# GpSimd in place of VectorE for the low parts of six projection weights in a two-layer attention kernel

## The reference, cut to what matters

```
h = modulate(rms_norm(x, norm1_g[i]), sh1, sc1)
hc = modulate(rms_norm(ctx, norm1_g[i]), csh1, csc1)
a_z, bq, bk, bv, cq, ck, cv = split_proj(h @ w_in[i])      # w_in[i]: 1024 x 2048
a_zc, bqc, bkc, bvc, cqc, ckc, cvc = split_proj(hc @ w_in[i])
...                       # roots, gains and rotations of bq, bk, cq, ck
s = einsum(q_c, k_c) ; p = softmax(s) ; pd = p[0] - lam * p[1] ; o = pd @ v   # "C" heads
out_b = window_attn_latent(q_b, k_b, v_b, k_bc, v_bc, b_sink[i])              # "B" heads
```

## Time and profile before

| | us |
|---|---|
| median of 3 runs (lowest, highest) | 1688.5 (1685.79, 1691.37) |
| the profiled execution, its own time | 1696.3 |
| its span in the profile | 1694.5 |
| PE busy | 1646.9 (97%) |
| DVE busy | 1213.6 (72%) |
| ACT busy | 880.1 (52%) |
| POOL busy | 200.2 (12%) |

### The profile page before, as it was taken

The page is one execution under the profiler, slowest core; times in us unless marked ns, Lnnn a source line. Parts: engine busy times, 40 slices in busy tenths (PEclk is TensorE's granted clock), DMA queues, the critical chain, the costliest instruction groups (busy, mean ns, idle before and its releaser), DMA issues.

```text
span 1694.5 us, 34323 instructions
## 1 busy us (share of the span) xinstructions
PE 1646.9 (97%) x14687; PEld 1470.6 (87%) x14687; DVE 1213.6 (72%) x2054; ACT 880.1 (52%) x1335; POOL 200.2 (12%) x124
## 2 busy tenths in 40 slices
PE   8999999999999999999989999999999998899999
PEld 7999988898999999997766888888887786699999
DVE  3374499687777786577766788876888778568864
ACT  5435645548546665445774444323433456656643
POOL 4303540000000110100000111100110100131100
PEclk9999999999999999999999999999999999999999
DMA  7655555354455554521202243363344322045544
GB/s 273 243 210 222 195 218 184 152 222 174 148 176 178 189 174 155 183 102 54 73 2 85 91 149 136 144 229 138 135 160 176 131 76 101 5 172 186 188 160 139
DMA packets 41128, 259.65 MB, mean 153 GB/s; under 512 B 4368, under 2 KB 7696, under 8 KB 14480
## 3 DMA queue, kind: packets, MB, share of 16 engines
q1 hardware_dynamic: 40976, 257.46, 42.3%
HBM read 256.39 MB, written 1.05 MB: 152 GB/s over the span
## 4 chain that ended last, share of the span: by engine, by line
PE 76%; DVE 17%; ACT 3%; DMA 2%; issue 2%; SPq 0%; DVEq 0%; ACTq 0%
PE acc_psum L197 22%; PE acc_psum L199 21%; PE acc_psum L198 21%; DVE w_low_sb L163 3%; DVE mod_products L324 2%; PE acc_psum L2511 2%; PE acc_psum L206 2%; DVE ring_sb L324 2%; PE acc_psum L2537 1%; DVE u_filtered L2064 1%; PE acc_psum L260 1%; ACT w_high_sb L152 1%; DMA ring_sb<-in_w_up 1%; ACT norm_rt_sb L2761 1%; PE acc_psum L1098 1%
## 5 line engine op out<-in xcount | busy, mean ns | idle before, releaser
L197 PE MATMUL acc_psum<-h_high_sb,w_high_sb 128*128 128x256 f32 (+1 forms) x2176 | 664.3, 305 | 4.5 <-DVE h_low_sb L486 2.6
L199 PE MATMUL acc_psum<-h_high_sb,w_low_sb 128*128 128x256 f32 (+1 forms) x2176 | 658.7, 303 | 0.0
L198 PE MATMUL acc_psum<-h_low_sb,w_high_sb 128*128 128x256 f32 (+1 forms) x2176 | 658.3, 303 | 0.0
L152 ACT ACTIVATE w_high_sb<-ring_sb 128x1024 fp32r<-128x1024 f32 (+2 forms) x412 | 386.9, 988 | 375.6 <-PE acc_psum L199 230.3
L163 DVE TENSOR_TENSOR w_low_sb<-ring_sb,w_high_sb 128x1024 fp32r<-128x1024 f32 (+1 forms) x358 | 391.0, 1134 | 109.9 <-ACT w_high_sb L152 100.3
L197 PEld LDWEIGHTS acc_psum<-h_high_sb,w_high_sb 128*128 128x128 f32 x2176 | 411.4, 189 | 33.0 <-issue 12.0
L198 PEld LDWEIGHTS acc_psum<-h_low_sb,w_high_sb 128*128 128x128 f32 x2176 | 410.8, 189 | 17.6 <-issue 0.5
L199 PEld LDWEIGHTS acc_psum<-h_high_sb,w_low_sb 128*128 128x128 f32 x2176 | 411.1, 189 | 17.2
L163 POOL TENSOR_TENSOR w_low_sb<-ring_sb,w_high_sb 128x1024 fp32r<-128x1024 f32 x54 | 131.9, 2465 | 682.0 <-ACT w_high_sb L152 681.9
L2064 DVE SCALAR_TENSOR_TENSOR u_filtered<-acc_psum,par_sb,u_filtered 128x255 f32<-128x255 f32 (+2 forms) x264 | 150.7, 571 | 58.3 <-ACT u_filtered L2201 40.3
L197 PE MATMUL acc_psum<-u_high,w_high_sb 128*128 128x256 f32 (+1 forms) x528 | 169.2, 320 | 3.3 <-DVE w_low_sb L163 2.8
(11 more groups left out here) (312 smaller groups left out, 1872.2 us busy)
## 6 DMA issues: line engine op xcount, KB each, us to landing
ring_sb<-in_w_in SPq DMA_DIRECT2D x68, 1024.0 KB, 6.4
ring_sb<-in_w_up SPq DMA_DIRECT2D x66, 1024.0 KB, 4.9
ring_sb<-in_w_down SPq DMA_DIRECT2D x48, 704.0 KB, 4.1
ring_sb<-in_w_ada SPq DMA_DIRECT2D x24, 1024.0 KB, 4.8
ring_sb<-in_w_ada_rows SPq DMA_DIRECT2D x24, 1024.0 KB, 4.8
ring_sb<-in_w_out SPq DMA_DIRECT2D x12, 1024.0 KB, 4.8
ring_sb<-in_w_br_hg SPq DMA_DIRECT2D x4, 1024.0 KB, 6.9
ring_sb<-in_w_br_ml SPq DMA_DIRECT2D x4, 1024.0 KB, 5.0
```

Source lines behind the costliest of these rows:

```text
L152: self.nc.scalar.activation(self.high[:, g % 2, piece], self.ring[:, c % RING, piece], ACT.Copy)\
L197: nc.tensor.matmul(out, sh, mh, start=start, stop=False)
L198: nc.tensor.matmul(out, sh, ml, start=False, stop=False)
L199: return nc.tensor.matmul(out, sl, mh, start=False, stop=stop)
```

## The change

In both attention layers the units g = 2 to 7 (7, 4, 2, 3, 1, 0) get the word "pool", and a block for POOL is added that runs their `split_low` in order. Unit g = 0 is still POOL's, g = 1 and g = 8 are still DVE's. DVE's calls stay in the code and do nothing for the six units. Nothing else changes: ACT, PE and SP have the same instructions in the same order.

```
         for i in range(LAYERS):
-            add("w_in_2", [8 * i + n for n in (6, 5, 7, 4, 2, 3, 1, 0)], "dve", "pool")
+            add("w_in_2", [8 * i + n for n in (6, 5)], "dve", "pool")
+            add("w_in_2", [8 * i + n for n in (7, 4, 2, 3, 1, 0)], "pool", "pool")
...
             sp.wait_ge(*ws_in.at(16))
 
+        @block.gpsimd
+        def _(pool):
+            for g in range(2, len(ORDER)):
+                core.split_low(pool, g0 + g, "pool")
+
         @block.tensor
```

## The result

The changed kernel takes 1708.2 us (median of 4 executions, 1704.3 to 1708.4), the kernel before 1689.9 us on the same chip (4 executions, 1685.8 to 1691.4): ratio 1.0102, 95% interval 1.0077 to 1.0126. It is slower, by about 1%. The forecast of 1701.8 us had the right sign and its range of 1689 to 1709 holds the time, but the time is 6.4 us above it, and 2.2 us above the 1697 to 1706 that the walk gave for itself.

A forecast was written before the change was run, and what follows sets the result against it. PE's matmuls bound the kernel; only 5.0 us of waits for DVE could be won. Place by place, 3.2 + 0 + 1.6 + 0.7 + 2.9 + 4.9 = 13.3 us on the 1688.5 us median gave 1701.8 us, range 1689 to 1709.

The forecast's parts named there:

- the walk: Both attention layers, DVE's timeline place by place: POOL's L163 hold DVE's instructions, 13.3 us slower, 1701.8 us; chance 0.58.
- D (relief): Both attention layers: all 5.0 us of PE's waits for DVE go and nothing is held, 1683.5 us; chance 0.04.
- C (only the pace): POOL and DVE do not hold each other off, slack covers POOL's pace: -3 to +0.5, 1688 us; chance 0.12.
- A (small instructions slip through, or their delay is covered): Only holds of long instructions cost, 3.2 + 2.9: +6.1 us, 1694.6 us; chance 0.16.
- B (pile-up): g = 4 and 5 also cost, 2.9 us a layer, other places hit at worst phase: +22, 1710.6 us; chance 0.10.
- the sum of 13.3 us: PE's added standing time over both attention layers, relief already taken off: 3.2 + 0 + 1.6 + 0.7 + 2.9 + 4.9.
- Layer 0, g = 2 and 3: Two POOL pairs hold DVE 9.5 us, L2934 ends 4.4 us later, PE stands 3.2 us at the transposes.
- Layer 0, g = 4 to 7: 0 at g = 4 and 5 (covered by waits for scores), 1.6 us at g = 6, 0.7 us at g = 7.
- Layer 1, g = 2 and 3: L2934 ends 4.4 us later, 1.5 us of cover before PE's transposes, PE stands 2.9 us.
- Layer 1, g = 6 and 7: Softmax chain, `mix` and the rotations of `keys_b` held; L2925 4.9 us late, 3.8 the other way, and PE waits.

The follow-up runs named there:

- the dummies: Kernel before, plus POOL products of two constant tiles into scratch that nobody waits for: 1733.4 us, ratio 1.0245; with memsets that only write instead: 1693.1 us, 1.0006.
- g = 6 and 7 alone: Changed kernel with only the low parts of units 1 and 0 left on POOL, the other units' back on DVE: 1696.3 us, ratio 1.0031 to the kernel before.
- g = 4 and 5 together: Changed kernel with only the low parts of units 2 and 3 left on POOL, the other units' back on DVE: 1691.9 us, ratio 1.0018 to the kernel before.
- the kernel with memsets: Kernel before, plus four POOL memsets of a 128 x 512 scratch tile for each high piece of g = 2 to 7: 1693.1 us, ratio 1.0006.
- the two kernels with fillers: Unused constant matmuls put in PE's waits: kernel before, three waits of layer 1, 1689.7 us, 0.9983; changed kernel, all long waits, 1698.7 us, 1.0047 to before.

## Why the prediction was right, and by how much it was off

The mechanism is the one predicted: what DVE is relieved of is less than what POOL's reading holds it up, and PE waits for DVE at the named places. The rivals fall. D (relief) and C (only the pace) are excluded by the sign and by the dummies. A (small instructions slip through, or their delay is covered) by the 2.28 us of a 128 x 1 instruction and by the 1.0031 of g = 6 and 7 alone; the 35 us that it took as free on DVE in each layer are 40 in layer 0. B (pile-up) gave nearly the timed size, but for another reason: g = 4 and 5 together cost 1.5 to 3 us and not 5.8, and the parts add up without a pile-up.

How the sum of 13.3 us fared, step by step. Net of the clock, as above, layer 0 is 187.3 us before and 191.9 after, layer 1 133.0 and 139.5. Other traces repeat this: 191.7 and 139.3 in the second trace of the changed kernel, 187.3 and 133.1 in that of the kernel with memsets.

- *Layer 0, g = 2 and 3*: 3.2 us predicted; 2.1 at the transposes and 0.2 at the low part measured. The four holds added 2.08 + 2.19 us for each unit, 8.5 us and not 9.5, since DVE's instruction comes to POOL's piece when it has run for 0.3 to 0.4 us; and the second piece of g = 2 was nearly in time. Counted from the layer's first L450 and net of the clock, L2940 ends 3.8 us later than L2934 did, where 4.4 was predicted.
- *Layer 0, g = 4 to 7*: 2.3 us predicted (0 + 1.6 + 0.7). `values` waits 2.5 us more, `turn` 0.6 us less. In sum layer 0 is 4.6 us longer, 5.5 predicted.
- *Layer 1, g = 2 and 3*: 2.9 predicted, 1.9 measured, for the same reason (L2940 is 3.2 us late and not 4.4).
- *Layer 1, g = 6 and 7*: 4.9 predicted. `turn` waits 3.6 us, where I had 4.1, and not the same two were held: the walk had L2962 (now L2968) held by the first piece and L2972 (now L2978) by the second. L2968 slipped through at 1412.00, 0.16 us ahead of POOL's start, and L2978 and `mix` were held in their place. For that case the walk had a stall of 1.4 us with `mix` alone held, which was too little, so that the 4.1 came nearly true is in part luck. The B transposes wait 4.4 us, and the 2.4 us of `values` are down to 0.2. The layer is 6.5 us longer, 7.8 predicted; less the 1.9 above, that leaves 4.6 for this step.

So the stalls came to 4.6 + 6.5 = 11.1 us where the sum had 13.3. The holds were sized 1 us too long for each pair of units in `keys_c`, and the rest was close.

What the sum did not have is a term: **the clock of TensorE behind the stalls**. Each us of wait was counted once. But the profile before already had it: its windows show a granted clock of 0.98 and 0.96, which nothing in the prediction used, and finer windows put part of it right behind the 2.4 us wait in layer 1, with 0.83 from 1415 to 1425 us:

```profile
1415.00:1425.00 10.00, 7.64 (x105) 7.06 (x104) 9.59 (x25) 6.01 (x11) 0.00 (x0) 0.83 0.24 75
```

Over all executions the changed kernel loses 15.6 us to the clock and the one before 11.1, 4.5 us more. Of the difference of the mean times (1706.6 over 8 executions, 1691.0 over 49: 15.6 us), 11.1 are the stalls, and 4.5 are left, as much. In the first result, 18.3 us, the medians of 4 executions each lie 1 to 2 us on the far side of these means. That every us at the lower clock costs a us is not shown: over the 49 executions of before the time rises by 0.78 us for each us lost (correlation 0.79), and the two kernels with fillers gained 0.5 and 0.6 us for each us of clock that came back, since part of the slow time lies in waits and fillers can overrun a wait by tenths of a us. At 0.5 to 1 us for each, the clock's part is 2.3 to 4.5 us of the 15.6, so the split is good to about 2 us. Nor is all of it placed: in the two traces of the changed kernel the attention layers lose 10.2 us to the clock, in the one trace shown of the kernel before 7.7 (2.6 and 5.1), and the rest of what is lost lies in stretches that the change does not touch and varies from execution to execution.

The two misses have opposite signs, stalls 2.2 us too large and a clock term of some 2 to 4.5 us left out. So part of the closeness of the time is luck.

The choice to hold the sum against the median of the runs shown, 7.8 us below the profiled execution, was right: on the profiled execution it would have given 1709.6, above all that was measured.

What stays open: why g = 4 and 5 cost 1.5 to 3 us without a new wait of PE in the trace. Its profiled execution, with 0.7 us net of the clock, is one of the quickest of its kernel (1685.9 us, median 1691.9), so it may not show what the others have.

## What to carry to other kernels

Before work is moved from VectorE to GpSimd, look whether both would read SBUF at the same time with VectorE on two-input instructions: relief is then paid back with nearly the whole of each GpSimd instruction (4.3 us for each 4.8 us here), and an idle GpSimd is no free engine. If it must be, cut GpSimd's instructions short (here that took the ratio from 1.0102 to 1.0044, still slower than before), or give it work that only writes, as the memsets here. And count a new stall of TensorE of 2 to 4 us, as these were, as more than its length, because the matmuls behind it may run at 1.2 GHz; dummy matmuls in unavoidable waits bought back 0.2 to 0.4% here.

## What the runs showed of the hardware that I had not expected

- The granted clock can fall behind waits of 2 to 4 us in a kernel whose PE is 97% busy. It does not behind each: in the changed kernel it is 1.00 from 750 to 765 us, around the 2.1 us wait at layer 0's C transposes, and falls behind the 1.9 us wait at those of layer 1. The fall from 1415 to 1425 us in the kernel before, at 0.83, stands for 1.7 us (10 x 0.17), and how many come varies from execution to execution: the mean clock of the kernel before went from 0.991 (1696.0 us, mean of 5 executions) to 0.996 (1688.0 us, mean of 6). It goes with most of the spread of its times. The Trainium skill, TensorE: Matmul & The Clock Gate, section "What's actually happening", has the throttled state as the default that activity releases; the traces here agree with the two levels, 0.12 and 0.21 us between starts of 128 x 256 matmuls.
- The smallest VectorE instructions are held like large ones (128 x 1: 0.22 to 2.28 us). And not only those that read two tiles: L657, a TENSOR_SCALAR that reads one tile in SBUF, went from 0.17 to 2.37 us beside POOL. It is one case, and no run was made for it.
- POOL's reads of constants, which no other engine's result hangs on, hold DVE like its reads of weights: 77 us of them cost 41 us of the kernel's time, the clock included, while some 50 us of memsets cost nothing that can be measured.
